# A two-layer hybrid recurrent decoder step: the four heads' samples on 128 partitions, row and column groups of the array, and a reordered weight stream

## The reference

```python
for t in tokens:                      # per head, state S is 128 x 128
    A: S = a_t (I - b_t k_t k_t^T) S + b_t k_t v_t^T;  o_t = S^T q_t      # gated delta, conv on q, k, v; q, k L2-normed
    B: S = gamma_h S + k_t v_t^T;                      o_t = S^T q_t      # retention, rotary q, k
    C: S = diag(f_t) S + k_t v_t^T, k_t = 1 - f_t;     o_t = S^T q_t      # HGRN2
o_n    = norm_over_head(o_n) * act(gate_n)                                # n = A, B, C
merged = sum_n sigmoid(x @ W_gate_n) * (o_n @ W_branch_n)
x = x + g1 * (merged @ W_out);  x = x + g2 * ((silu(h @ W_g) * (h @ W_u)) @ W_down)
# outputs: y of both groups, and the new states of the prompt (1 x 4 heads) and of the samples (8 x 4 heads) for A, B, C
```

## Time and profile before

| | us |
|---|---|
| median of 3 runs | 3214.1 (3212.15 to 3222.64) |
| the profiled execution | 3212.1, its span 3210.2 |
| PE busy | 2922.2, 91% of the span |
| PE weight loads (PEld) | 2681.7, 84% |
| DVE busy | 1228.9, 38% |
| ACT busy | 472.3, 15% |
| POOL busy | 1400.5, 44% |
| mean granted TensorE clock | 0.903 of full speed |

### The profile page before, as it was taken

One profiled execution on the slowest core, in us unless ns is written; L12 is line 12 of the kernel. 1 busy time (PEld: TensorE's weight loads), 2 busy tenths in 40 slices (PEclk: granted clock), 3 DMA queues, 4 the chain that ended last, 5 costly groups with the idle time before them and its releaser, 6 DMA issues. The chain is left out here.

```text
span 3210.2 us, 48470 instructions
## 1 busy us (share of the span) xinstructions
PE 2922.2 (91%) x20570; PEld 2681.7 (84%) x20570; DVE 1228.9 (38%) x1572; ACT 472.3 (15%) x944; POOL 1400.5 (44%) x728
## 2 busy tenths in 40 slices
PE   6998998889998879999889989989899988799997
PEld 3977896877995879999859779968689968799996
DVE  2545412313353384333235444132225335732332
ACT  2221122111112110000023111221110121100000
POOL 1322232343533547776523222313355336477774
PEclk9987897986997989999999789969889979899998
DMA  7520011211411312222275100112113113122222
GB/s 276 183 88 27 27 47 40 83 56 40 121 45 43 114 60 91 83 91 85 63 266 172 57 27 28 53 50 59 56 60 112 47 37 127 60 90 82 93 80 74
DMA packets 126319, 264.11 MB, mean 82 GB/s; under 512 B 9616, under 2 KB 68496, under 8 KB 124304
## 3 DMA queue, kind: packets, MB, share of 16 engines
q1 hardware_dynamic: 126096, 260.93, 25.5%
HBM read 239.72 MB, written 21.17 MB: 81 GB/s over the span
## 5 line engine op out<-in xcount | busy, mean ns | idle before, releaser
L627 PE MATMUL gemm_psum<-h_hi_lo,w_hi_lo 128*128 128x272 f32 x12000 | 1710.9, 302 | 66.2 <-DVE h_hi_lo L1114 38.8
L627 PEld LDWEIGHTS gemm_psum<-h_hi_lo,w_hi_lo 128*128 128x128 f32 x12000 | 1619.4, 199 | 176.7 <-issue 139.8
L600 POOL TENSOR_TENSOR w_hi_lo<-w_raw,consts 128x1024 fp32r<-128x1024 f32 (+3 forms) x362 | 617.4, 1706 | 1744.5 <-PE gemm_psum L627 1618.8
L602 POOL TENSOR_TENSOR w_hi_lo<-w_raw,w_hi_lo 128x1024 fp32r<-128x1024 f32 (+3 forms) x362 | 784.0, 2166 | 28.4
L1725 ACT ACTIVATE tiles<-gemm_psum 128x544 f32<-128x544 f32 (+1 forms) x188 | 116.3, 623 | 1304.8 <-PE gemm_psum L627 1303.6
L627 PE MATMUL gemm_psum<-ffn_hi_lo,w_hi_lo 128*128 128x272 f32 x2112 | 266.8, 288 | 0.0
L627 PEld LDWEIGHTS gemm_psum<-ffn_hi_lo,w_hi_lo 128*128 128x128 f32 x2112 | 266.4, 188 | 0.0
L627 PE MATMUL gemm_psum<-o_hi_lo,w_hi_lo 128*128 128x272 f32 x1152 | 161.0, 296 | 16.3 <-POOL w_hi_lo L602 16.3
L627 PEld LDWEIGHTS gemm_psum<-o_hi_lo,w_hi_lo 128*128 128x128 f32 x1152 | 152.4, 194 | 18.1 <-POOL w_hi_lo L602 17.4
L1708 DVE TENSOR_TENSOR tiles<-gemm_psum,tiles 128x544 f32<-128x544 f32 x44 | 31.9, 725 | 319.6 <-PE gemm_psum L627 319.6
L1714 DVE TENSOR_TENSOR ffn_hi_lo<-tiles,ffn_hi_lo 128x544 fp32r<-128x544 f32 x44 | 119.8, 2722 | 1.5
(11 more groups left out here) (225 smaller groups left out, 2413.2 us busy)
## 6 DMA issues: line engine op xcount, KB each, us to landing
w_raw<-in_w_gu SPq DMA_DIRECT2D x88, 512.0 KB, 3.5
tiles<-in_w_ada SPq DMA_DIRECT2D x64, 512.0 KB, 4.1
w_raw<-in_w_merge SPq DMA_DIRECT2D x48, 384.0 KB, 3.0
w_raw<-in_w_first SPq DMA_DIRECT2D x34, 512.0 KB, 3.6
w_raw<-in_w_ret SPq DMA_DIRECT2D x32, 512.0 KB, 3.4
w_raw<-in_w_hg SPq DMA_DIRECT2D x32, 512.0 KB, 3.5
w_raw<-in_w_merge SPq DMA_DIRECT2D x48, 256.0 KB, 2.7
w_raw<-in_w_dn SPq DMA_DIRECT2D x32, 384.0 KB, 3.1
```

What stands on the lines that cost most here:

```text
L600: pool.tensor_tensor(hi, src, ones[:, 0:1].broadcast_to([P, words]), ALU.mult).then_inc(hi_done, 1)
L602: pool.tensor_tensor(lo, src, hi.bitcast(F32), ALU.subtract).then_inc(split_done, 1)
L627: mm = pe.matmul(GP[:, 2 * (tile % 2) + h, 0:HALF], whl[:, n % 2, a, j * P:(j + 1) * P], rhs[:, b, step, h * HALF:(h + 1) * HALF], start=s ...
```

## The change

1. **Samples of the four heads on 128 partitions.** Partition 32 h + s holds sample column s of head h. Tiles that were 32 x (4 x 32) become one 128 x 128 tile with a mask that is zero between heads, and every four instructions of 32 rows or columns become one. DVE and ACT work on the same number of columns as before.
2. **`sample_outputs`**: `read_states` multiplies all states of a head by its 32 query columns, output in column group h (partitions 32 h), 512 columns; ACT copies the two (mixer A: four) banks to SBUF; `pick` takes from the result, with 8 products of 16 columns, what belongs to each sequence.
3. **`sample_states`**: for a half (4 sequences), head h in row group h and bank h, four products in a row; all four heads by half instead of two heads ahead of the spreads and two behind.
4. **Sums and spreads**: `four_sums` writes the four heads to four column groups (32 output columns each), `four_spreads` reads four row groups (32 rows each) into the four banks; DVE multiplies four heads at once (128 x 4 x 272), ACT copies and `low_part` work on halves of the tokens with all heads.
5. `rows_of` comes ahead of the state products in `out_norm`, and the scale of q moves from `rows_of` into the DVE multiplication.
6. **Stream**: gdn_z stands ahead of ret_v, and Z_END is now the start of ret_v, so mixer A's prompt part can draw on 12 tiles instead of 16 and mixer A's sample part on 8 instead of 4. `LEVEL_FILL = (1, 1, 1)`, and DVE's `gdn_level` puts both `gdn_add` ahead of the level's fills.

```diff
-LEVEL_FILL = (2, 1, 1)
+LEVEL_FILL = (1, 1, 1)
...
+    block("gdn_z", "first", 13, 4)
     block("ret_v", "ret", 8, 4)
-    block("gdn_z", "first", 13, 4)
...
-Z_END = BASE["ret_g"]
+Z_END = BASE["ret_v"]
...
-                def spread(i, at):
-
+                def four_sums(sq, j, first, last):
+
+                    if first:
+                        acquire(0)
+                        acquire(1)
+                    k.next(sig("square_ready"), H)
                     for h in range(2):
-                        b = 2 * (at % 2) + h
-                        acquire(b)
-                        pe.matmul(B[:, b, 0:HALF], sel[0:8, i, :], RWO[0:8, h * HALF:(h + 1) * HALF],
-                                  start=True, stop=True).then_inc(full[b], 1)
+                        for i in range(H):
+                            mm = pe.matmul(B[32 * i:32 * i + 32, h, 0:HALF], hot[:, j, :], sq[i][:, h * HALF:(h + 1) * HALF],
+                                           start=first, stop=last, skip_group_check=True)
+                    if last:
+                        mm.then_inc(sig("sums_done"), 1)
+
+                def four_spreads(j, half):
+
+                    for i in range(H):
+                        acquire(i)
+                        pe.matmul(B[:, i, 0:HALF], spr[32 * i:32 * i + 32, j, :],
+                                  RWO[32 * i:32 * i + 32, half * HALF:(half + 1) * HALF], start=True, stop=True
+                                  ).then_inc(full[i], 1)
...
+                def read_states(bank, queries):
+
+                    for half in range(2):
+                        acquire(bank + half)
+                        for h in range(H):
+                            mm = pe.matmul(B[32 * h:32 * h + 32, bank + half, :], queries[:, h * SW:(h + 1) * SW],
+                                           S8[:, h, 4 * half:4 * half + 4, :], start=True, stop=True, skip_group_check=True)
+                        mm.then_inc(full[bank + half], 1)
+
+                def pick(out, read, fresh):
+
+                    o4 = out.rearrange("p (h b t) -> p h b t", h=H, b=NS)
+                    for b in range(NS):
+                        mm = pe.matmul(o4[:, :, b, :], read[:, b, :], pick_seq[:, :, b, :], start=fresh,
+                                       stop=fresh or b == NS - 1, skip_group_check=True)
+                    return mm
...
-                def sample_states(n, h, limit):
+                    read_states(0, flat(0))
+                    fill(3, limit)
+                    k.peek(free[0])
+                    k.peek(free[1])
+                    acquire(2)
+                    pe.matmul(hcol(2, 0), val, sc, start=True, stop=False, skip_group_check=True)
+                    pick(hcol(2, 0), QS[n][0], False).then_inc(full[2], 1)
+
+                def sample_states(n, half):
 
                     ke = (small, rsm, hsm)[n]["kend"]
-                    k.next(sig("masked_values"))
-                    for half in range(2):
-                        acquire(2 + half)
-                        pe.matmul(B[:, 2 + half, :], ke[0:SW, h, :], UM[n][h % 2][0:SW, 4 * half:4 * half + 4, :],
-                                  start=True, stop=True).then_inc(full[2 + half], 1)
-                        fill(1, limit)
+                    if half == 0:
+                        k.next(sig("masked_values"))
+                    for h in range(H):
+                        p0 = 32 * h
+                        acquire(h)
+                        pe.matmul(B[:, h, :], ke[p0:p0 + 32, 0, :], UM[n][p0:p0 + 32, 4 * half:4 * half + 4, :],
+                                  start=True, stop=True).then_inc(full[h], 1)
...
-                    for i in range(H):
-                        square_sum(i, H, hot[:, i, :], 8, sq_o[n])
-                        fill(1, limit)
-                    for h in range(2):
-                        sample_states(n, h, limit)
+                    fill(2, limit)
+                    four_sums(sq_o[n], 0, True, True)
+                    fill(3, limit)
                     k.next(sig("rows_ready"))
-                    for i in range(H):
-                        spread(i, i)
+                    for half in range(2):
+                        four_spreads(0, half)
                         fill(2, limit)
-                    for h in range(2, H):
-                        sample_states(n, h, limit)
+                    fill(1, limit)
+                    for half in range(2):
+                        sample_states(n, half)
+                        fill(4, limit)
...
-                for at, i in enumerate((4, 5, 6, 7, 0, 1, 2, 3)):
-                    spread(i, at)
-                    fill(1, Z_END)
+                for j in (1, 0):
+                    for half in range(2):
+                        four_spreads(j, half)
+                        fill(2, Z_END)
```

More of the change, by code:

```diff
@@ L659, in tiles_of @@
                         return [brt[:, first + h, cols(c)] for h in range(H)]
-                    return [SMP[:, at + h, :] for h in range(H)]
+                    return [flat(at)]
                 def square_sum(i, count, lhs, rows, sq):
@@ L1733, in square, with squares, root @@
                     f(slot, tile, ACT.Square).then_inc(sig("square_ready"), 1)
-                def root(rows, scale):
-                    k.peek(sig("square_slot_free"), 2)
-                    f(halves(RWO[0:rows, :]), B[0:rows, 0:2, 0:HALF], ACT.Sqrt, scale=scale, bias=epsc[0:rows, :]
-                      ).then_inc(sig("root_ready"), 1)
+                def squares(tiles, slots):
+                    for tile, slot in zip(tiles, slots):
+                        f(slot, tile, ACT.Square).then_inc(sig("square_ready"), 1)
+                def root(scale, sums=None):
+                    if sums:
+                        k.next(sig(sums))
+                    else:
+                        k.peek(sig("square_slot_free"), 2)
+                    f(halves(RWO[:, :]), B[:, 0:2, 0:HALF], ACT.Sqrt, scale=scale, bias=epsc).then_inc(sig("root_ready"), 1)
                 def high_parts(shift):
```

532 lines of the change are left out of this document (285 added, 247 removed).

## The result

Kernel before 3214.15 us (median of 4 runs, 3212.15 to 3222.64), changed kernel **2911.76 us** (2910.56 to 2917.19, 4 runs): ratio 0.9058, 95% interval 0.9038 to 0.9078, so 302 us less. The profiled execution has a span of 2910.7 us at a granted clock of 0.954 (before 3210.2 and 0.903). Lines of the changed kernel are numbered anew: 807 is now 859, 678 now 718 (spreads), 669 now 709 (sums), 735 now 786 (state products), 723 now 736 (reads) and 744 (picks), 655 now 683 (transposes), 823 now 881, 829 now 887, 843, 851 and 858 now 901, 909 and 916, 627 now 655 (stream).

A forecast was written before the change was run, and what follows sets the result against it. PE was taken as the bound, busy 2922 of 3210 us, moved by its work, idle time and clock. Stage savings sum to 124 us a layer, 248 in two, less 2 for POOL: 2966 us, own range 2925 to 3000, whole 2890 to 3040.

The forecast's parts named there:

- Slots of a round: Rounds of four products, counted in one record's time: 3 slots plus 0.2 us, 0.9 us (272 columns) or 1.5 us (512).
- program order: Rival: a product's second record waits for its first, 5 slots a round, 21 us a layer more, 3008 us; chance 0.10.
- Clock loss: Low-clock time left after idles in L2 spreads, mixer A and norms B and C: 4.5, 6, 9 and 6 us.
- L2 spreads: Stage 215.3 to 255.1, 39.8 us with 10 steps: would take 27.8 us, -12 a layer.
- Levels: Stage 255.1 to 479.5: steps move out, a rope-tile wait goes, another comes; -3 us a layer, bounds -15 and +8.
- Mixer A: Its samples and norm, 479.5 to 573.8, 94.3 us with 32 steps: would take 62.4 us, -32 a layer.
- Sample outputs of B and C: 12 us at clock 0.72 in B become two read rounds, picks and rest: -8.3 us, the same for C.
- Norm B: Stage 699.8 to 772, 72.2 us with 23.5 steps: would take 42.5 us, -30 a layer.
- Norm C: Stage 983.4 to 1044.8 and 1.8 us behind: would take 37 us, -26 a layer.
- Clock up and full overlap: Rival: none of the 25.5 us clock loss, 2 slots a round; 36 us a layer less, 2894 us; chance 0.12.
- Nothing overlaps: Rival: 5 slots more in all rounds, 53 us a layer, and about 15 of clock, 3102 us; chance 0.07.
- Slower: Rival: in spread, sum, read and state stages nothing overlaps and the clock stays low; +182 us a layer, 3330; chance 0.03.

The follow-up runs named there:

- one_row_group: Changed kernel with all four products of each spread or state round reading rows 0 to 31, so row groups cannot overlap; 2981.6 us.
- whole_rows: Changed kernel with each spread and state product reading all 128 rows, so again none overlap; 2926.2 us.
- tall_before: Kernel before, with spreads contracting over 128 rows in place of 8 and state products over 128 in place of 32; 3117.8 us.
- z_first: Changed kernel with mixer A's gate tiles ahead of the rope tiles in the stream; 2905.4 us.
- no_groups: Changed kernel with spreads and states all on rows 0 to 31, and sums and reads on the same output rows, so nothing overlaps; 3036.3 us.
- one_column_group_2: Changed kernel with the four products of each sum or read round writing the same output rows, so column groups cannot overlap; 2980.4 us.
- best: Changed kernel with mixer A's gate tiles first, stream steps moved from drains to waits, 2, 1, 1 steps a level, three value tiles allowed there; 2843.0 us.
- long_first_fill: Changed kernel with 2, 1 and 1 steps in a level and only two value tiles allowed ahead of mixer A's end; 2894.9 us.

## Why the prediction was right, and what was mis-sized

The direction, the mechanism (packing, overlap, clock) and the whole range held. The forecast was 54 us too high, and the time fell below its own range of 2925 to 3000. By its own steps, first layer:

- **Slots of a round.** Taken 3 slots and 0.2 us (0.9 and 1.5 us), bounds 2 and 8; measured 2 slots and 0.2 us for rows (0.67 and 1.07), 0.53 and 0.89 for columns. The sum over all rounds with their updates was 45.4 us; measured are 9.9 + 6.7 + 7.5 + 17.3 = 41.4 (busy time of lines 718, 709, 736 and 786 with the last one's waits, halved), since the second state rounds wait for DVE bank by bank. 4 us. The earlier trace rows had said as much: 2.4 records saved at each of three changes leave 8 - 7.2, less than the 2 slots that are the floor; I read it rightly and then took a careful 3. The rival "program order" is dead: records of four products start within 0.02 us. Of the Trainium skill's two factors ("TensorE: Matmul & The Clock Gate", Part 3), the trace has a state round 3.03 / 1.07 = 2.8 times as fast as serial products over whole rows, a little below its 3.07 for four row groups (against serial products of 32 rows at clock 1.00, in one_row_group, it is 3.62 / 1.07 = 3.4); four column groups gave 3.7 times, where the page has 2.38 for three.
- **Clock loss.** Taken 4.5 + 6 + 9 + 6 = 25.5 us; by length x (1 - clock) of the rows above 3.5 + 1.5 + 3.3 + 4.2 = 12.5. **This is the largest mis-sized term**, 13 of the 29 us a layer (153 against 124). I had let the loss follow the idle times; one_row_group, whole_rows and tall_before show that lone products with few rows have a part in it as well, and the change leaves none among the spreads and state products. The expectation "0.8 where 0.58 stood" for norm B gave 0.85.
- **Start.** Conv sums -4, measured -7; where the other 3 us lie was not looked up.
- **L2 spreads** -12, measured -14.5 in the rest; wait at the first turn 5.2, measured 4.31, cause shown by z_first. The gate rows' wait was 6.59, not 5.1.
- **Levels** -3, measured +0.5, inside the bounds -15 and +8. The waits at line 909 came as forecast (9.7 us a layer, measured 16.7 / 2 = 8.4, three of up to 3.6). Not seen: the -15 was to be had with one more step in the first fill.
- **Mixer A** -32, measured -45 with a wait of 2.19 us behind it at mixer B's first transposes (forecast 2.3): -43. The first spread waited 2.24 us (forecast 2.3), the update all but nothing (forecast 2.5).
- **Sample outputs of B and C** -8.3 each; rests 11.7 to 3.8 and 12.1 to 3.8, so -8 and -8.3.
- **Norm B** -30, measured -42.5: clock 9 against 3.3, and the hg_f tile's wait 0.93 in place of 3.3. **Norm C** -26, measured -28; its first spread waited 4.05 us, not 2.3.
- **What would show it.** Clock 0.954 (0.96 said) and line 735's waits for ACT gone, as said; idle time 266 us, over the 200 to 250 said; PE busy -277, not -170, as the clock's gain lies in the busy time.
- **Rivals.** "Clock up and full overlap" (2894) was nearer in mechanism than the forecast: full overlap came, half of the clock loss stayed. "Nothing overlaps" was priced at +136 us above the forecast, and no_groups is +125 (give or take 21) above the real kernel: the price held, its base did not. "Slower" (+182 a layer) asked for a low clock through all serial stages; no_groups, where nothing overlaps, is 62 us a layer above the real kernel.

## What to carry to other kernels

Price a group of products by the slots that remain when all overlap, and keep a larger figure for the range, not for the forecast, when a row of the trace shows the overlap. Ask of small products how many rows they use, and not only how long they take: filling the empty rows of the spreads and state products alone gave the kernel before 96 us (filled with other data; rows of zeros were not run). Count stream steps as a budget that each wait bids for, and look which tile ends at each place, and on which engine it lands, before moving them.

## What the hardware showed that was not expected

- **Rows and the clock.** A stretch's clock is the mean of two levels, 1.2 GHz (0.50) and 2.4 GHz (1.00). With the same records and the same wait ahead (2.25 us at the first spread) norm B stands at 0.75 with 32 rows one by one, 0.85 with four groups side by side, 1.00 with 128 rows.
- **A change of rows has a price of its own.** At clock 1.00 a spread of 8 rows or a state product of 32 rows between stream steps costs 0.4 us more than one of 128 rows, and a serial round of eight such records costs the same 0.4 once (no_groups: 6.82 us with four steps, against 8 x 0.427 + 4 x 0.75 = 6.41). In groups a state round with four steps takes 4.28 us, where two slots and the steps are 3.85: four products pay the price once.
- **Columns.** In one_column_group_2 all four reads of a round, and three of its four sums, write 32 of 128 output columns one by one; the clock of the whole stayed at 0.953.
- **DVE beside POOL.** Low parts and rope's sine product on DVE take two operands from SBUF. Two low parts in norm A of the kernel after, and two in norm C, with POOL's split beside the latter:

```profile
475.69 2.49 DVE L1498 TENSOR_TENSOR o_hi_lo<-tiles,o_hi_lo 128x1088 fp32r<-128x1088 f32 x2 [0.54 <-DVE tiles L1483]
```

```profile
875.06 5.31 DVE L1498 TENSOR_TENSOR o_hi_lo<-tiles,o_hi_lo 128x1088 fp32r<-128x1088 f32 x2 [0.54 <-DVE tiles L1483]
```

```profile
873.92 1.89 POOL L628 TENSOR_TENSOR w_hi_lo<-w_raw,consts 128x1024 fp32r<-128x1024 f32 x1 [11.40 <-PE gemm_psum L655]
875.89 3.32 POOL L630 TENSOR_TENSOR w_hi_lo<-w_raw,w_hi_lo 128x1024 fp32r<-128x1024 f32 x1
```

The sine product (least, median and longest ns of the first layer's eight):

```profile
L1206 DVE TENSOR_TENSOR tiles<-tiles,consts x8: 707/2902/2928, 227.5 to 366.5; 128x544 f32<-128x544 f32 x8
```

The reciprocal, with one operand, takes 3.55 us in either company. A tile's end frees both the slab that POOL splits and the operands that DVE takes, so the two meet nearly every time, and the 2.9 us that I took from the earlier trace rows as the price of an operation are 0.7 of work and 2.2 of waiting. The one of the eight that takes 707 ns is the one with no split beside it; the other seven start 0.04 us into POOL's line 630 and end 0.58 us behind it. In best two start 1.43 us into it and take 1.53. So DVE waits for the whole of POOL's instruction. The Trainium skill, "SBUF — State Buffer", "Who interferes with whom", has this rule: a DVE instruction with two SBUF inputs contends with a GpSimd instruction that reads SBUF, over a shared port pair that is "an exclusive lock". The trace agrees. No run here took the overlap away by itself, so how much of the waits at line 909 it causes stays open.
- **Also open:** how the 9.5 us of mixer A in long_first_fill divide between the late root and the slow low parts.
